# Four weight blocks prepared by GpSimd in the up stage, and another order of products and loads in the down stage

## The reference, cut to what matters

```
u = h @ w_up                                   # 1024 -> 2 x 2816
uc = causal depthwise conv of width 3 over u, + b_conv
a, g = split(uc)
x = x + g2 * ((silu(a) * g) @ w_down)          # 2816 -> 1024
```

## Time and profile before

| | us |
|---|---|
| median of 3 runs (lowest, highest) | 3030.19 (3029.31, 3030.48) |
| the profiled execution | 3033.03 |
| its span, first to last instruction | 3031.1 |
| TensorE busy | 2901.1 (96%) |
| VectorE busy | 1946.3 (64%) |
| ScalarE busy | 1266.7 (42%) |
| GpSimd busy | 565.6 (19%) |

### The profile page before, as it was taken

The page is one execution under the profiler, slowest core; times in us unless marked ns, Lnnn a source line. Parts: engine busy times, 40 slices in busy tenths (PEclk is TensorE's granted clock), DMA queues, the critical chain, the costliest instruction groups (busy, mean ns, idle before and its releaser), DMA issues.

```text
span 3031.1 us, 49224 instructions
## 1 busy us (share of the span) xinstructions
PE 2901.1 (96%) x17179; PEld 2510.9 (83%) x17179; DVE 1946.3 (64%) x3067; ACT 1266.7 (42%) x2542; POOL 565.6 (19%) x576
## 2 busy tenths in 40 slices
PE   7999999999999999999998999999999997999998
PEld 5878888887777888888888999999999995777776
DVE  2300016733998999795667777777877778767665
ACT  4611112223776888454564333333332323333322
POOL 3310003312666776220110000000000020000000
PEclk8999999999999999999999999999999998999999
DMA  6322225544522251796655444444666664555554
GB/s 217 114 76 73 72 70 159 157 132 112 132 58 58 60 104 35 237 329 195 209 168 183 150 150 150 150 152 170 189 199 211 215 225 156 162 172 168 172 168 150
DMA packets 341130, 459.07 MB, mean 151 GB/s; under 512 B 68738, under 2 KB 221512, under 8 KB 338278
## 3 DMA queue, kind: packets, MB, share of 16 engines
q1 hardware_dynamic: 327432, 416.48, 43.7%
q0 software_dynamic: 12208, 40.46, 4.1%
q10 hardware_dynamic: 1332, 0.06, 0.0%
HBM read 285.43 MB, written 171.48 MB: 151 GB/s over the span
## 4 chain that ended last, share of the span: by engine, by line
PE 41%; DVE 8%; DMA 5%; issue 3%; ACT 2%; SPq 1%; DVEq 0%; ACTq 0%
PE facc L2918 26%; PE eacc L2897 6%; PE dacc L3050 3%; PE facc L3050 2%; DMA dpart<-act_d 2%; DVE dres L2584 1%; PE mpT L3073 1%; DMA x_d<-dres 1%; DVE dT L2573 1%; PE mpm L3082 1%; PE eyT L2880 0%; PE mpS L3092 0%; DVE dT_plain L2565 0%; PE mpN L3108 0%; DMA y_out<-dres 0%
## 5 line engine op out<-in xcount | busy, mean ns | idle before, releaser
L767 PE MATMUL pacc<-pring,h1H 128*128 128x512 f32 x1360 | 431.6, 394 | 3.4 <-ACT h1H L326 3.4
L2918 PE MATMUL facc<-fright,fsums 128*128 128x416 f32 x2112 | 418.1, 353 | 10.7 <-ACT facc L1965 6.8
L2918 PEld LDWEIGHTS facc<-fright,fsums 128*128 128x128 f32 x2112 | 398.1, 189 | 16.9 <-issue 8.7
L1123 DVE TENSOR_TENSOR_SCAN aC<-aB,aC,a 128x512 f32<-128x512 f32 (+3 forms) x326 | 363.0, 1113 | 12.1 <-ACT aB L1079 1.1
L1183 POOL TENSOR_TENSOR aS<-aS,aC 128x512 f32<-128x512 f32 (+3 forms) x326 | 334.5, 1034 | 152.6 <-DVE aC L1123 146.0
L2918 PE MATMUL facc<-fright,fwH 128*128 128x416 f32 x1056 | 291.4, 357 | 12.7 <-DVE fU L2397 10.8
L767 PEld LDWEIGHTS pacc<-pring,h1H 128*128 128x128 f32 x1360 | 256.7, 189 | 56.2 <-ACT h1H L326 3.5
L767 PE MATMUL pacc<-pring,h1L 128*128 128x512 f32 x640 | 248.0, 389 | 0.0
L2918 PEld LDWEIGHTS facc<-fright,fwH 128*128 128x128 f32 x1056 | 201.3, 191 | 17.4 <-issue 12.2
L1203 PE MATMUL a_z<-ak,aq 128*128 128x512 f32 (+2 forms) x616 | 199.4, 405 | 0.6 <-DMA ak<-qk_T 0.6
L368 ACT ACTIVATE pstage<-pacc 128x512 f32<-128x512 f32 x112 | 66.6, 595 | 308.5 <-PE pacc L767 308.3
(11 more groups left out here) (389 smaller groups left out, 5778.3 us busy)
## 6 DMA issues: line engine op xcount, KB each, us to landing
sums_d<-fsums SPq DMA_DIRECT2D x88, 512.0 KB, 3.0
fsums<-sums_d SPq DMA_DIRECT2D x88, 512.0 KB, 4.8
fraw<-w_up SPq DMA_DIRECT2D x66, 512.0 KB, 4.1
proj_out<-pstage SPq DMA_DIRECT2D x119, 256.0 KB, 2.0
dres<-x_d SPq DMA_DIRECT2D x92, 256.0 KB, 3.3
qk_T<-pturn POOLq DMA_DIRECT2D x68, 256.0 KB, 3.1
mwa<-w_ada SPq DMA_DIRECT2D x16, 1024.0 KB, 6.1
dpart<-act_d SPq DMA_DIRECT2D x32, 512.0 KB, 4.5
```

The source lines that it names most:

```text
L767: op = mm_(acc[:, n % NB], h[:, kk, tok(t)], weight(q, w), start=(j == 0), stop=(j == len(order) - 1))
L1123: v.tensor_tensor_scan(buf[:, a:b][:, ::-1], part(B, RB, n)[:, ::-1], nought[:, 0:width(n)], buf[:, b:b + 1], ALU.mult, ALU.add).then_inc( ...
L2918: mm = nc.tensor.matmul(bank, a[:, kk], b[:, kk], start=(begins and kk == 0 and m == 0), stop=(kk == count - 1 and m == 2), skip_group_che ...
```

## The change

Three things are changed.

1. Four pairs of weight blocks (pairs 0 to 3) are gated and summed by GpSimd during the narrow half of the up stage, from its pair 8 on (`AHEAD_FROM`). SyncE loads their rows, and stores the seven finished blocks of each to a new DRAM tensor (`wd_ahead`). The down stage loads finished blocks from it for pairs 0 to 3, and again for pairs 11 and 12 (which are pairs 0 and 1 once more); these are then only split. `first_blocks` and `first_rest` are gone.
2. P4 is the third product of a unit instead of the last, in a bank of its own (f) that it starts afresh. So there is a third addition of a first product (`add_first`), and P7's bank is added to two outputs: output 1 is P5 and P7, output 2 is P4 and P7, output 3 is P5 and P3, output 0 is P2 alone. The order of the high and low parts on ScalarE and VectorE follows.
3. On SyncE, a unit's activation blocks are asked for earlier, the second half ahead of all stores. The raw rows' load stands behind the store of output 2.

```diff
-    PRODUCTS = ("P1", "P5", "P6", "P2", "P7", "P3", "P4")
...
+    PRODUCTS = ("P1", "P5", "P4", "P6", "P2", "P7", "P3")
+    AHEAD, AHEAD_FROM = 4, 8
...
+            def load_ahead(m):
+                if m == 0:
+                    sp.wait_ge(t_ready, 8)
+                    sp.wait_ge(b_low, 6)
+                    sp.wait_ge(done["SG"], NF)
+                    sp.dma_start(ahead_gate[:], d["mods"][0:1, gate_at:gate_at + D].to_broadcast([P, D])).then_inc(ahead_in, 16)
+                for a in range(2):
+                    sp.dma_start(ahead_rows[:, a], d["w_down"][(2 * m + a) * P:(2 * m + a + 1) * P, :]).then_inc(ahead_in, 16)
+
+            def store_ahead(m):
+                sp.wait_ge(cell_sum, 4 * m + 4)
+                sp.dma_start(d["wd_ahead"][m, 0], ahead_rows[:, 0, 0:W5]).then_inc(ahead_stored, 16)
+                sp.dma_start(d["wd_ahead"][m, 1:3].rearrange("n p c -> p n c"),
+                             ahead_rows[:, 1].rearrange("p (n c) -> p n c", c=W5)).then_inc(ahead_stored, 16)
+                sp.dma_start(d["wd_ahead"][m, 3:].rearrange("n p c -> p n c"), ahead_sums[:]).then_inc(ahead_stored, 16)
+                sp.wait_ge(ahead_stored, 48 * m + 48)
...
             def load_act(w, e):
                 if w >= 2:
-                    sp.wait_ge(left_low, 7 if w == 2 else 7 * (w - 1 + e))
+                    sp.wait_ge(left_sum, 4 if w == 2 else 4 * w - 4 if e else 4 * w - 1)
+                    sp.wait_ge(left_low, 7 if w == 2 else 7 * w - 7 if e else left_of(LEFT_LOWS, "S1", w - 1))
...
+            for i in range(AHEAD_FROM, NF - 3):
+                narrow_loads(i)
+                if i == AHEAD_FROM:
+                    load_ahead(0)
+                m, odd = divmod(i - AHEAD_FROM - 2, 2)
+                if 0 <= m < AHEAD and not odd:
+                    store_ahead(m)
+                    if m + 1 < AHEAD:
+                        load_ahead(m + 1)
+                    else:
+                        load_first("B11", ahead_in)
+                        load_first("T1", ahead_in)
...
+            load_first("T4", cell_in[0])
             store_narrow(NF - 2)
+            sp.wait_ge(done["P6"], UP)
+            load_first("T2", cell_in[1])
+            sp.wait_ge(done["P2"], UP)
+            sp.wait_ge(cell_in[0], 16)
+            load_first("B21", cell_in[0])
+            sp.wait_ge(done["P7"], UP)
+            sp.wait_ge(cell_in[1], 16)
+            load_first("T3", cell_in[1])
             sp.wait_ge(done["P3"], UP)
+            sp.wait_ge(cell_in[0], 32)
+            load_first("B22", cell_in[0])
...
                     store_sample()
                 if w + 2 < UNITS:
+                    load_act(w + 2, 1)
+                if COMING.get(w + 1, 0) in (NK, NK + 1):
+                    sp.wait_ge(out_ready, 4 * w)
+                    load_cells(COMING[w + 1])
+                store_out(w, 0)
+                if w + 2 < UNITS:
                     load_act(w + 2, 0)
-                store_out(w, 0)
+                if w + 1 < UNITS:
+                    load_res(w + 1, 0)
+                store_out(w, 1)
+                store_out(w, 2)
                 if w + 1 in COMING and w > 0:
                     load_rows((w + 1) // 2)
-                store_out(w, 1)
-                if w + 1 < UNITS:
-                    load_res(w + 1, 0)
-                store_out(w, 2)
                 if w + 1 < UNITS:
                     load_res(w + 1, 1)
+                store_out(w, 3)
                 if w == 1:
                     sp.wait_ge(ends_taken, 1)
                     for t in range(2):
...
                     sp.wait_ge(ends_stored, 32)
                 if w + 1 < UNITS:
                     load_res(w + 1, 2)
-                if w + 2 < UNITS:
-                    load_act(w + 2, 1)
-                store_out(w, 3)
-                if w + 1 < UNITS:
                     load_res(w + 1, 3)
...
+            def gate_ahead(m):
+                pool.wait_ge(ahead_in, 16 + 32 * m + 32)
+                for a in range(2):
+                    nc.gpsimd.tensor_tensor(ahead_rows[:, a], ahead_rows[:, a], ahead_gate[:], ALU.mult).then_inc(cell_gated, 1)
+
+            def sum_ahead(m):
+                one, other, at = ahead_rows[:, 0], ahead_rows[:, 1], ahead_sums
+                left_, right_ = slice(0, W5), slice(W5, D)
+                pool.wait_ge(cell_gated, 2 * m + 2)
+                at_least(pool, ahead_stored, 48 * m)
+                nc.gpsimd.tensor_tensor(at[:, 0], one[:, right_], one[:, left_], ALU.subtract).then_inc(cell_sum, 1)
+                nc.gpsimd.tensor_tensor(at[:, 2], other[:, right_], one[:, right_], ALU.subtract).then_inc(cell_sum, 1)
+                pool.wait_ge(cell_sum, 4 * m + 1)
+                nc.gpsimd.tensor_tensor(at[:, 1], other[:, right_], at[:, 0], ALU.subtract).then_inc(cell_sum, 1)
+                pool.wait_ge(cell_sum, 4 * m + 3)
...
-            def add_five(w, j):
-                dve.wait_ge(done["P5"], UP + w + 1)
+            def add_first(w, j):
+                bank, product = (down_f, "P4") if j == 2 else (down_e, "P5")
+                dve.wait_ge(done[product], UP + w + 1)
                 dve.wait_ge(res_in[j], 16 * w + 16)
-                v.tensor_tensor(res_of(w, j), res_of(w, j), down_e, ALU.add).then_inc(five_added, 1)
+                v.tensor_tensor(res_of(w, j), res_of(w, j), bank, ALU.add).then_inc(first_added, 1)
 
             def add_out(w, j):
-                dve.wait_ge(done[("P2", "P7", "P3", "P4")[j]], UP + w + 1)
-                dve.wait_ge(*((res_in[j], 16 * w + 16) if j in (0, 3) else (five_added, 2 * w + (2 if j == 1 else 1))))
-                bank = (down_a, down_b, down_c, down_b)[j]
+                dve.wait_ge(done[("P2", "P7", "P7", "P3")[j]], UP + w + 1)
+                dve.wait_ge(*((first_added, 3 * w + j) if j else (res_in[0], 16 * w + 16)))
+                bank = (down_a, down_b, down_b, down_c)[j]
...
-                banks = {"P1": down_a, "P5": down_e, "P6": down_b, "P2": down_a, "P7": down_b, "P3": down_c, "P4": down_b}
+                banks = {"P1": down_a, "P5": down_e, "P6": down_b, "P2": down_a, "P7": down_b, "P3": down_c, "P4": down_f}
...
-                        pe.wait_ge(*((five_added, 2 * w) if w else (e_taken, UP)))
+                        pe.wait_ge(*((first_added, 3 * w) if w else (e_taken, UP)))
...
-                        pe.wait_ge(out_ready, 4 * w + 2)
...
+        k.scratch("wd_ahead", [4, 7, P, W5])
```

More of the change, by code:

```diff
@@ L1905, in _ @@
             store_h2(final)
-            first_blocks()
+            for m in range(AHEAD):
+                gate_ahead(m)
+                sum_ahead(m)
         @block.scalar
@@ L2535, in first_low_of @@
             def first_low_of(name):
-                dve.wait_ge(cell_high, HIGHS[0].index(name) + 1)
-                dve.wait_ge(cell_sum, {"T1": 1, "T2": 2, "B22": 3}.get(name, 0)) if name in ("T1", "T2", "B22") else None
-                if name == "B11":
-                    dve.wait_ge(cell_sum_pool, 1)
+                dve.wait_ge(cell_high, FIRST_HIGHS.index(name) + 1)
                 top, low, own = first_cells(name)
-                if name == "B21":
-                    for n in range(FIRST):
-                        op = v.tensor_tensor(low[:, n], b21_rows[n], top[:, n].bitcast(F32), ALU.subtract)
-                else:
-                    op = v.tensor_tensor(low, own, top.bitcast(F32), ALU.subtract)
@@ L2546, in first_low_of @@
-                op.then_inc(cell_low, 1)
+                v.tensor_tensor(low, own, top.bitcast(F32), ALU.subtract).then_inc(cell_low, 1)
             def gate_row(a, n):
-                dve.wait_ge(down_gate_in, 48)
+                dve.wait_ge(down_gate_in, 16)
                 dve.wait_ge(raw_rows_in, 48 * event(n) + 48)
@@ L2596, in down_slot @@
                 coming = COMING.get(w - w % 2)
-                sums_ = w % 2 == 0 and w > 0 and coming is not None
+                sums_ = w % 2 == 0 and w > 0 and coming is not None and not stored_ahead(coming)
                 lows = w % 2 and coming is not None
@@ L2647, in down_slot @@
                     product(UP - 1, NARROW)
-                    for a in range(2):
-                        gate_row(a, coming)
-                    for name in ("T1", "T3", "T2", "T4"):
-                        cell_sum_of(name, coming)
                 if w == 1:
@@ L3049, in down_unit @@
                         for m, (a, b) in enumerate(((high, b_high), (high, b_low_), (low, b_high))):
-                            mm = nc.tensor.matmul(banks[name], a[:, i], b, start=(name in ("P1", "P5") and i == 0 and m == 0),
+                            mm = nc.tensor.matmul(banks[name], a[:, i], b, start=(name in ("P1", "P5", "P4") and i == 0 and m == 0),
                                                   stop=(i == len(WINDOW[w]) - 1 and m == 2), skip_group_check=True)
```

275 lines of the change are left out of this document (113 added, 162 removed).

## The result

The kernel after takes 3122.2 us (median; 3121.5 to 3123.1), the kernel before 3029.9 us in the same session: 1.031 times as long, with a 95% interval of 1.029 to 1.032. The forecast was 3057 us with a range of 3022 to 3088. The direction was right, the size 3.4 times too small: +27.2 us were predicted, +92 came.

A forecast was written before the change was run, and what follows sets the result against it. TensorE was seen losing about 75 us of the down stage to seed copies, output additions and slowed clock; terms summed to +27.2 on 3033.0 us, 3060.2, less 2.8 for the median: 3057 us, range 3022 to 3088.

The forecast's parts named there:

- End of the up stage, -8.3: Last up pairs: block and gate loads queued ahead of the next up weights leave this place, saving 8.3 us.
- GpSimd beside the up stage, +15: Narrow half of the up stage: GpSimd's gating slows VectorE, and what exceeds its idle time reaches TensorE; 15 us added.
- the upper bound: Narrow half: 15.6 us of contention plus a late weight load of 4.37 us in each of four pairs; 33 us.
- the contention row: Up stage profile: two VectorE tap instructions took 2.83 us under GpSimd instead of 0.91; two thirds of that time lost.
- the likeliest case: Whole kernel: the main forecast of 3057 us, chance 0.65, alone spanning 3036 to 3080 us.
- Waits of P4, P7 and the seeds: Down stage: TensorE's waits for seed copies (27.7 us) and output additions (25.8 us) nearly all go.
- The sample's rows, 8.2 us a time: Ten even units from 2 on: rows queued behind later stores land late; 6.5 us wait plus 1.7 us clock each.
- Units 0 and 1: Start of the down stage: less VectorE work gives 46.5 us, late rows make it 50, against 57.5; -7.5 us.
- Units 18 to 23: Last down units: 89.2 + 8.9 for the rows + 3 left over = 101.1 us against 109.8; -8.7 us.
- A: Down stage, faster rival: the rows' transfer stays hidden, so only gains remain; 2975 us, chance 0.08.
- B: No-change rival: rows' waits come without clock loss, and GpSimd's work costs the up stage nothing; 3026 us, chance 0.14.
- C: Up stage, slower rival: VectorE loses all of GpSimd's time and clock drops; 35 us in place of 15; 3077 us, chance 0.13.

The follow-up runs named there:

- e8_vector_gates: As e5, but VectorE, not GpSimd, gates and sums the four blocks stored ahead, their DMAs spread over three up pairs from pair 5; 2977.7 us.
- e5: Kernel after, with the sample's rows issued ahead of all stores and SyncE waiting for the stored blocks' landing one up pair later; 2991.4 us.
- e6: As e5, with GpSimd gating and summing only 8 columns in blocks 1 to 3 (output wrong there); 2982.7 us, one run.
- e4: Kernel after, with GpSimd gating and summing only 8 columns in blocks 1 to 3, DMAs and waits kept; 3116.5 us, one run.
- e1: Kernel after, with the sample's rows issued directly behind the store of output 0, as in the kernel before; 3063.5 us.

## Why the prediction was right and wrong

- **End of the up stage, -8.3:** right to the tenth; over the last three pairs 56.1 us became 47.8, and e8_vector_gates has this gain alone. For the cause that was given, the loads ahead of the up weights, the trace of before speaks: VectorE sat idle 8.10 us until 2468.51 for the high part of the weights that left the queue behind them. No run moved these loads alone, and GpSimd's first blocks left this place with them.
- **GpSimd beside the up stage, +15:** the first step that failed. This term of the sum came to +33.6, the upper bound as the prediction had written it, and for the reason given there: SyncE "waits until it has landed". I took the value of the contention row and put SyncE's wait for the stores, 8 to 10 us at each of four blocks, at nothing in the likeliest case. The runs say that both costs are real and not additive. Contention, with the queue open, is 15.7 us for three of the four blocks (e5 against e6) and 18.3 for all (e5 against e8, whose DMAs are also spread), close to the 15; the queue's wait with little contention is 33.6 - 2.0 = 31.6 (e4); both together are 33.6.
- **Waits of P4, P7 and the seeds:** right. From unit 3 on nothing waits for them, and a unit of four pairs takes 19.6 us.
- **The sample's rows, 8.2 us a time:** the step that decides, and the second that failed: right in mechanism, too small. Measured 11.0 a time (358.9 - 281.8 us over seven of them, after against e5). Counted as the prediction did, from P7's end at 2739.1: the activation part was issued at 5.3 us, not 4.8, and landed 5.8 us later, not 4.5; other transfers, two stores the nearest, stood directly ahead of the rows. 11.1 - 2.8 is the 8.3 us of wait, where 6.5 were forecast. The landing of a row of before was used as a constant though the change altered what travels beside it. (The 0.16 us from P7's end to the third left sum stands in no row; here it was 0.3.) The rest, 2.7 us, is clock, against 1.7: the sample's own 16 matmuls ran at 1.2 GHz too (1.93 us for 1.07), which I had not counted.
- **Units 0 and 1:** predicted 50 us, measured 61.0. The rows for unit 2 came 11.9 us late instead of about 3, and P4 in its early place waited 4.4 us for a left block. Without the late rows (e5) the stretch is 49.8 us where it was 57.5 before, a relief of 7.7 us, not the 11 that made 46.5 of it. P4's new wait of 4.4 us stands in it; that this wait is what took the rest no run shows.
- **Units 18 to 23:** -3.1 instead of -8.7. The last sample's wait was 13.6 us, not the 7.2 that its 8.9 holds: in that unit `load_cells`, seven block loads, stands ahead of the store of output 0, the residual's load ahead of the rows stood 3.5 us for that store's landing (it left at 3043.97), and the activation part left 9.4 us behind P7's end in place of 5.3. The sum had neither at that place.
- **Rivals:** A's condition was false, but its price has the size of what the rows cost: ahead of all stores, and with the queue open in the up stage, the kernel is at 2991 us where A gave 2975. B's conditions were false: each of the ten long waits was followed by half clock (1.93 us for the sample's 1.07), and the up stage did pay for GpSimd's work. C's term for the narrow half, 35 us, came true in size by luck, not in reason: GpSimd's work beside VectorE costs 16 to 18.

Of the 63 us by which the span's growth (90.2) exceeds the forecast's (27.2), 20.7 lie in units 3 to 17, 18.6 in the narrow half, 11.0 in units 0 and 1, and the rest in smaller pieces. So the range was missed because both large terms were placed at the row of one cause, and SyncE's queue, with what travels in it, added to each.

## What to carry to other kernels

When a transfer is moved in a queue, or the work behind it is reordered, count its slack anew from the consumer: what must be finished before the issue, what travels beside it, and which product still lies behind the releasing event. A wait for a store's landing in a queue that also loads the critical operand is a stall of that operand; issue the store, go on, and wait one iteration later. And an engine that has 3 to 5 us idle in each iteration may take on work more cheaply than an idle engine with which it has to take turns.

## What the runs showed of the hardware that was not expected

- A short wait can cost nearly as much clock as a long one. A sample wait of 3.3 us in e1 cost 5.4 us a time (319.4 - 281.8 over seven), one of 8.3 us cost 11.0: 2.1 and 2.7 us beyond the wait. It doesn't each time: at the same product of unit 1, behind waits of 2.91 and 2.90 us, nine matmuls took 2.33 us in e5 and 3.68 in e6.

```profile
2546.37 2.33 PE L3054 MATMUL facc<-dB,dA 128*128 128x512 f32 x9 [2.91 <-DVE dres L2594]
```

```profile
2530.70 3.68 PE L3056 MATMUL facc<-dB,dA 128*128 128x512 f32 x9 [2.90 <-DVE dres L2596]
```

- A landing time grew by half with other transfers beside it: from 4.3 to 6.4 us for the same 1.05 MB and activation part.
- GpSimd beside VectorE: 2.35 us for a 128x1024 gating, of which VectorE does two in 2.35 us. The first subtraction of each block took 2.13 us and the three behind it 1.27 to 1.29 in the kernel after, though all have 512 columns; the view of the tile (ns, min/median/max):

```profile
L1911 POOL TENSOR_TENSOR dahead_rows<-dahead_rows,dahead_gate x8: 2338/2353/2408, 2304.4 to 2424.7; 128x1024 f32<-128x1024 f32 x8
L1918 POOL TENSOR_TENSOR dahead_sums<-dahead_rows x4: 2132/2132/2135, 2309.3 to 2427.1; 128x512 f32<-128x512 f32 x4
L1919 POOL TENSOR_TENSOR dahead_sums<-dahead_rows x4: 1262/1268/1282, 2311.4 to 2429.2; 128x512 f32<-128x512 f32 x4
```

The first one stands beside VectorE's low part of the up weights, at all four blocks. At the second, VectorE's instruction ends at 2349.18 and the subtraction 1.12 us later:

```profile
2346.93 2.25 DVE L2402 TENSOR_TENSOR fwL<-fraw,fwH 128x1024 fp32r<-128x1024 f32 x1 [9.59 <-ACT fwH L2013]
```

```profile
2348.17 2.13 POOL L1918 TENSOR_TENSOR dahead_sums<-dahead_rows 128x512 f32<-128x512 f32 x1
```

So GpSimd waits for VectorE too, inside its instruction, and the low part took 2.25 us for 1.23 behind GpSimd's gating. How far the stores' size sets the rows' landing stays open.
